# A streaming encoder layer on eight cores: mixer and attention of the next tile list-scheduled beside the FFN of this one

## What is computed

```python
u, v, gb, gc, xin = split(x @ w_in)            # 5 x 512
v    = layernorm(v, per head of 128)
a    = u * (w_s[h] @ v + b_s[h])               # mixing inside a block of 128 frames, masked
conv = causal width-3 convolution of gc * xin
x = layernorm(ALPHA * x + concat(a, gb * conv) @ w_out)
q = x @ w_q                                    # cross-attention into 256 memory tokens
p = softmax(q @ mem_k.T / 16)
x = layernorm(ALPHA * x + (p @ mem_v) @ w_mem_o)
x = layernorm(ALPHA * x + (silu(x @ w_gate) * (x @ w_up)) @ w_down)
```

## Time and profile before

| | |
|---|---|
| median of 3 runs (lowest, highest) | 4941.5 us (4804.48, 5052.2) |
| profiled execution: its own time | 4957.0 us is its span, slowest core (core 1); the fastest core took 4873.2 |
| TensorE matmul busy | 4037.4 us, 81% |
| TensorE weight load busy | 2823.9 us, 57% (beside the matmuls) |
| VectorE, ScalarE, GpSimd busy | 2130.4, 1153.5, 302.3 us |
| mean granted clock, core 1 | 0.842 |
| DMA | 610.47 MB, mean 123 GB/s |

### The profile page before, as it was taken

How to read it: one execution, slowest core, us unless ns; L and a number is a source line. 1 busy time by engine, 2 the same in 40 slices (tenths; PEclk the granted TensorE clock), 3 DMA queues, 4 the chain that set the end, 5 groups by cost and what they waited for, 6 DMA issues and landing times.

```text
span 4957.0 us, 77469 instructions; the slowest of 8 cores (4873.2 to 4957.0 us)
## 1 busy us (share of the span) xinstructions
PE 4037.4 (81%) x27048; PEld 2823.9 (57%) x27048; DVE 2130.4 (43%) x4671; ACT 1153.5 (23%) x2511; POOL 302.3 (6%) x275
## 2 busy tenths in 40 slices
PE   3476888797979788897879798897979989799794
PEld 2254565565657565665657575655657556575563
DVE  0340544435353545445353545445154441544423
ACT  1020231413222231313122221313122031220312
POOL 1210000000000000000000000000000000000000
PEclk8688889898989899898989899897777777777775
DMA  8899333242424243332424243331423314233135
GB/s 172 136 171 161 124 120 141 88 147 74 177 86 158 94 145 107 115 137 77 158 86 169 83 149 111 116 136 73 149 73 130 115 69 147 76 128 115 64 138 212
DMA packets 137192, 610.47 MB, mean 123 GB/s; under 512 B 26877, under 2 KB 50589, under 8 KB 79724
## 3 DMA queue, kind: packets, MB, share of 16 engines
q1 hardware_dynamic: 90716, 564.31, 32.5%
q0 software_dynamic: 46096, 41.21, 6.6%
HBM read 603.51 MB, written 69.09 MB: 136 GB/s over the span
## 4 chain that ended last, share of the span: by engine, by line
PE 63%; DVE 14%; issue 8%; POOL 4%; ACT 4%; another core or an unknown queue 3%; DMA 3%; DVEq 1%; ACTq 0%; POOLq 0%; SPq 0%
PE bank L710 13%; PE bank L680 12%; PE bank L685 12%; PE bank L545 8%; PE bank L458 6%; PE bank L621 5%; POOL rstd L431 3%; PE bank L650 2%; PE bank L409 2%; ACT PT L643 2%; DVE xbuf L462 2%; DVE acc L516 1%; DMA wsc<-w_in 1%; DMA ring<-wsc 1%
## 5 line engine op out<-in xcount | busy, mean ns | idle before, releaser
L685 PE MATMUL bank<-F,ring 128*128 128x256 bf16 (+1 forms) x5808 | 792.3, 283 | 45.0 <-DMA ring<-wsc 39.0
L680 PE MATMUL bank<-F,ring 128*128 128x256 bf16 (+1 forms) x5808 | 798.7, 285 | 24.6 <-ACT sg L691 21.9
L545 PE MATMUL bank<-F,ring 128*128 128x256 bf16 (+1 forms) x4224 | 534.0, 294 | 206.2 <-DVE acc L516 198.7
L693 DVE TENSOR_TENSOR hT<-bank,sg 128x256 bf16<-128x256 f32 (+1 forms) x726 | 302.1, 418 | 907.8 <-PE bank L685 768.8
L710 PE MATMUL bank<-ring,hT 128*128 128x512 bf16 (+1 forms) x2860 | 672.9, 401 | 18.7 <-DMA ring<-wsc 15.8
L685 PEld LDWEIGHTS bank<-F,ring 128*128 128x128 bf16 x5808 | 583.7, 103 | 136.4 <-issue 49.0
L680 PEld LDWEIGHTS bank<-F,ring 128*128 128x128 bf16 x5808 | 587.9, 103 | 119.2 <-issue 28.2
L545 PEld LDWEIGHTS bank<-F,ring 128*128 128x128 bf16 x4224 | 434.3, 106 | 303.4 <-issue 224.1
L412 ACT ACTIVATE F<-bank 128x512 bf16<-128x512 f32 (+1 forms) x390 | 231.0, 594 | 1526.3 <-PE bank L409 1510.9
L710 PEld LDWEIGHTS bank<-ring,hT 128*128 128x128 bf16 (+1 forms) x2860 | 291.4, 102 | 393.5 <-issue 168.9
L409 PE MATMUL bank<-ident,xbuf 128*128 128x128 f32 (+1 forms) x1560 | 269.2, 334 | 291.8 <-DVE xbuf L448 234.8
(11 more groups left out here) (135 smaller groups left out, 3111.4 us busy)
## 6 DMA issues: line engine op xcount, KB each, us to landing
ring<-wsc SPq DMA_DIRECT2D x446, 1024.0 KB, 5.5
xbuf<-x_prompt SPq DMA_DIRECT2D x16, 2048.0 KB, 12.6
y_prompt<-xbuf SPq DMA_DIRECT2D x64, 512.0 KB, 2.9
ring<-wsc SPq DMA_DIRECT2D x51, 512.0 KB, 5.2
wsc<-w_gate POOLq DMA_DIRECT2D x5, 1024.0 KB, 108.3
wsc<-w_up POOLq DMA_DIRECT2D x5, 1024.0 KB, 92.5
wsc<-w_down POOLq DMA_DIRECT2D x5, 1024.0 KB, 127.8
wsc<-w_in POOLq DMA_DIRECT2D x16, 256.0 KB, 5.3
```

The lines of the kernel that those rows point to most:

```text
L545: op("tensor", lambda e, bk=bk, g=g, kc=kc, rg=rg: e.matmul(bk[:, 0:Tn], lhsT=rg[:, kc * 512 + g * 128:kc * 512 + (g + 1) * 128], rhs=F0[: ...
L680: op("tensor", lambda e, bkg=bkg, m=m, kc=kc, rgg=rgg, rl=rl: e.matmul(bkg[:, 0:Tn], lhsT=rgg[:, kc * rl + m * 128:kc * rl + (m + 1) * 128 ...
L685: op("tensor", lambda e, bku=bku, m=m, kc=kc, rgu=rgu, rl=rl: e.matmul(bku[:, 0:Tn], lhsT=rgu[:, kc * rl + m * 128:kc * rl + (m + 1) * 128 ...
L693: op("vector", lambda e, bku=bku, sgs=sgs, f=f: e.tensor_tensor(out=hT[:, f, cs], in0=bku[:, 0:Tn], in1=sgs, op=ALU.mult), reads=[bbu2, bs ...
```

## The change

The kernel is rewritten around the same arithmetic.

- **Order.** Operations are recorded with a duration, a priority and their buffers; `Sched.order()` then plays a list schedule and fixes from it, before the program is built, each engine's order. Part A of a tile (mixer and attention) has priority from t - 0.3 on, part B (the FFN) of tile t from t + 1, so that part A of tile t+1 stands among the matmuls of part B of tile t. Each part has its own weight ring (3 and 4 slots) and its own 4 PSUM banks.
- **Width.** All matmuls on a prompt tile stream 512 columns (the mixing inside blocks: 128).
- **Memory.** Once at the start, `precompute` folds the keys into the query weights and the values into the output weights, per group: the scores are then one projection of x of width 1,024 (`scores`), and after the softmax (`norm_p`) one projection gives the output. `w_q`, `K`, `V` and `w_mem_o` are no longer touched in the tiles.
- **Transposes.** x arrives a second time, already turned, as an input of its own (`x_prompt_t`), loaded by a cast DMA from GpSimd. The other two transposes of a tile are a bf16 copy by ScalarE and four DMA transposes on SyncE (`to_feature`, 128 x 1,024 bf16 each, 256 KB), into F0 (for the scores) and F2 (for the FFN).
- **Weights.** In the first use a piece is cast from the float32 input straight into its ring slot and stored from there to `wsc`; later uses read `wsc`. The input's pieces are laid out so that each partition's 4,096 columns are contiguous.
- **Sample.** The 64 sample frames go through tile 0's stages on the same weight pieces.
- The spatial bias, the layer norm of v and the convolution are rearranged (bias folded into one table, normalisation on ScalarE).

```diff
+    def order(self):
...
+            o = heapq.heappop(ready[e])[2]
...
+            if o.dma:
+                occ = 1.0 if e == "gpsimd" else 0.08
+                start = max(t + occ + 0.6, dma_free)
+                dma_free = start + o.nbytes / 330e3
+                fin = dma_free + 1.8
+            else:
+                occ = o.dur
+                if e == "scalar" and o.table is not None:
+                    if table is not None and o.table != table:
+                        occ += 1.4
+                    table = o.table
+                fin = t + occ
...
+        NRA, NRB = 3, 4
+        ring = {"A": [T("ra%d" % i, [128, 4096], BF16) for i in range(NRA)],
+                "B": [T("rb%d" % i, [128, 4096], BF16) for i in range(NRB)]}
...
+        pool = {"A": [0, 1, 2, 3], "B": [4, 5, 6, 7]}
...
+        def c_mm(n, cols):
+            return n * max(0.056, (cols + 6) / 2400.0)
...
+            if name in sidx and name in stored:
+                src = wsc[sidx[name]]
+                op("sync", lambda e: e.dma_start(out=t[:, 0:nco], in_=src[:, 0:nco]), [buf("wsc_" + name)], [b],
+                   dma="r%s%d" % (r, i), nbytes=256 * nco, dprio=dprio)
+            else:
+                src = wp[widx[name]]
+                op("gpsimd", lambda e: e.dma_start(out=t[:, 0:nco], in_=src[:, 0:nco]), [], [b],
+                   dma="f%s%d" % (r, i), nbytes=512 * nco, dprio=dprio)
+                if name in sidx:
+                    dst = wsc[sidx[name]]
+                    op("sync", lambda e: e.dma_start(out=dst[:, 0:nco], in_=t[:, 0:nco]), [b], [buf("wsc_" + name)],
+                       dma="w%s%d" % (r, i), nbytes=256 * nco, dprio=dprio)
+                    stored.add(name)
+            return t, b
...
+        def load_x(t):
+            i = t % 2
+            op("gpsimd", lambda e: e.dma_start(out=F0[:], in_=xpT[:, t]), [], [buf("F0_%d" % s) for s in range(4)],
+               dma="xt", nbytes=1 << 21, dprio=-0.25)
+            op("sync", lambda e: e.dma_start(out=xbuf[i][:], in_=xp[t * TT:(t + 1) * TT, :].rearrange("(s p) d -> p s d", p=128)),
+               [], [buf("x%d_%d" % (i, s)) for s in range(4)], dma="x%d" % i, nbytes=1 << 21, dprio=-0.1)
...
-        def transposes_to_feat(xb_i, subs, SP, c0, FT, b_FT):
-            for j, s in enumerate(subs):
-                for g in range(2):
-                    bk, bb = next_bank()
-                    for c4 in range(4):
-                        c = g * 4 + c4
-                        op("tensor", lambda e, bk=bk, s=s, c=c, c4=c4: e.transpose(
-                            bk[:, c4 * SP:(c4 + 1) * SP], xbuf[xb_i][0:SP, s, c * 128:(c + 1) * 128], ident[0:SP, 0:SP]),
-                           reads=[b_xb[xb_i][s], buf("ident")], writes=[bb])
-                    op("scalar", lambda e, bk=bk, j=j, g=g: e.activation(
-                        out=FT[:, g * 4:(g + 1) * 4, c0 + j * SP:c0 + (j + 1) * SP],
-                        in_=bk[:, 0:4 * SP].rearrange("p (c t) -> p c t", c=4), func=AF.Copy),
-                       reads=[bb], writes=[b_FT])
...
+        def resid(bk, bb, xv, bx, half, SP, i):
+
+            sl = slice(half * 512, (half + 1) * 512)
+            V(lambda e: e.scalar_tensor_tensor(out=xv[:, sl], in0=xv[:, sl], scalar=ALPHA, in1=bk[0:SP, :],
+                                               op0=ALU.mult, op1=ALU.add), [bb, bx[half]], [bx[half]], 512)
+            V(lambda e: e.bn_stats(out=stat[i][0:SP, half, :], in_=xv[:, sl]), [bx[half]], [buf("stat%d" % i)], 512)
+
+        def ln_apply(xv, bx, SP, li, i):
+            V(lambda e: e.bn_aggr(out=mv[i][0:SP, 0, :], in_=stat[i][0:SP, 0:2, :].rearrange("p a b -> p (a b)")),
+              [buf("stat%d" % i)], [buf("mv%d" % i)], 12)
+            rsqrt_stats(i, SP, 1)
+            V(lambda e: e.scalar_tensor_tensor(out=xv, in0=xv, scalar=mv[i][0:SP, 0, 0:1], in1=lng[li][0:SP, :],
+                                               op0=ALU.subtract, op1=ALU.mult), bx + [buf("mv%d" % i), buf("lng%d" % li)], bx, 1024)
+            V(lambda e: e.scalar_tensor_tensor(out=xv, in0=xv, scalar=rs[i][0:SP, 0:1], in1=lnb[li][0:SP, :],
+                                               op0=ALU.mult, op1=ALU.add), bx + [buf("rs%d" % i), buf("lnb%d" % li)], bx, 1024)
+
+        def to_feature(xv, bx, SP, dst, b_dst):
+
+            j = rot("xb", NXB)
+            A(lambda e: e.activation(out=xb[j][0:SP, :], in_=xv, func=AF.Copy), bx, [buf("xb%d" % j)], 1024)
+            op("sync", lambda e: e.dma_start_transpose(out=dst, in_=xb[j][0:SP, :]), [buf("xb%d" % j)], [b_dst],
+               dma="tr%d" % j, nbytes=1 << 19)
...
+                    MM([(bk[:], rg[:, k * 512 + cc * 128:k * 512 + (cc + 1) * 128], F0[:, k, :], k == 0, k == 7) for k in range(8)],
+                       [buf("F0_%d" % s) for s in range(4)] + [brg], [bb], 512)
+                    A(lambda e, bk=bk, ch=ch: e.activation(out=F1[:, ch, :], in_=bk[:], func=AF.Exp, scale=1.0 / 16.0),
+                      [bb], [buf("F1_%d" % ch)], 512, table="exp")
+                norm_p(F1, "F1_", h, TT)
+        def norm_p(FT, bn, h, n):
+            bk, bb = bank("A")
+            MM([(bk[:, 0:n], ones_bf[:], FT[:, 2 * h + mc, :], mc == 0, mc == 1) for mc in range(2)],
+               [buf("ones"), buf(bn + str(2 * h)), buf(bn + str(2 * h + 1))], [bb], n)
+            A(lambda e: e.activation(out=rden[:, 0:n], in_=bk[:, 0:n], func=AF.Ln), [bb], [buf("rden")], n, table="exp")
+            A(lambda e: e.activation(out=rden[:, 0:n], in_=rden[:, 0:n], func=AF.Exp, scale=-1.0), [buf("rden")], [buf("rden")], n, table="exp")
+            for mc in range(2):
+                V(lambda e, mc=mc: e.tensor_tensor(out=FT[:, 2 * h + mc, :], in0=FT[:, 2 * h + mc, :], in1=rden[:, 0:n], op=ALU.mult),
+                  [buf("rden"), buf(bn + str(2 * h + mc))], [buf(bn + str(2 * h + mc))], n)
...
+                        MM([(bk[:, i * 256:(i + 1) * 256], rg[:, (4 * hp + 2 * i + dc) * 512 + kk * 128:(4 * hp + 2 * i + dc) * 512 + (kk + 1) * 128],
+                             KT[z][:, 4 * hp + 2 * i + dc, :], dc == 0, dc == 1) for i in range(2) for dc in range(2)],
+                           [brg, b_KT[z]], [bb], 256)
...
+        def run_A(tiles, t):
+            def at(f):
+                S.prio = t + f - OFF
+            p_main = tiles[-1]
+            at(0.0)
+            rg, brg = piece("A", "in_v")
+            for c in tiles:
+                in_proj_v(c, rg, brg)
+            for m in range(4):
...
+                at(0.65 + 0.1 * hp)
...
+                at(0.86 + 0.07 * half)
...
+        def run_B(tiles, t):
+            n = NF // 2
+            for j in range(n):
+                S.prio = t + 1.0 + 0.6 * j / n
+                rg, brg = piece("B", "gu%d" % j)
+                for c in tiles:
+                    gate_up(c, j, rg, brg)
...
+                    S.prio = t + 1.6 + 0.2 * half + 0.06 * kp
```

More of the change, by code:

```diff
@@ L1 @@
 import contextlib
+import heapq
 import numpy as np
@@ L40, in __init__, with op @@
         self.sig = 0
-        self.dma = dma
+        self.dma = stream is not None
         self.stream = stream
         self.cnt = 0
+        self.dur = dur
+        self.prio = prio
+        self.nbytes = nbytes
+        self.seq = seq
+        self.left = 0
+        self.est = 0.0
+        self.fin = 0.0
+        self.succ = []
+        self.table = table
 class Sched:
+    LAT = 0.20
+    LAT_TO_PE = 0.45
     def __init__(self, nc):
         self.nc = nc
[L48 to L56, removed]
+        self.ops = []
+        self.prio = 0.0
+    def op(self, eng, fn, reads=(), writes=(), dma=None, dur=0.1, nbytes=0, table=None, dprio=0.0):
+        o = Op(eng, fn, dma, dur, self.prio + dprio, nbytes, len(self.ops), table)
         deps = []
@@ L84, in emit @@
     def emit(self, final_wait_eng="sync"):
         nc = self.nc
+        q = self.order()
+        streams = {}
         for e in QUEUES:
-            for o in self.q[e]:
+            for o in q[e]:
+                if o.dma:
+                    streams.setdefault(o.stream, []).append(o)
+        total = {}
+        for s, os_ in streams.items():
+            os_.sort(key=lambda o: o.seq)
+            for i, o in enumerate(os_):
+                o.cnt = 16 * (i + 1)
+            total[s] = 16 * len(os_)
@@ L88, in emit @@
+        for e in QUEUES:
+            for o in q[e]:
                 best = {}
@@ L103, in emit @@
             c = 0
[L104 to L107, removed]
+            for o in q[e]:
+                if not o.dma and o.signal:
                     c += 1
@@ new lines, in to_feature, with prompt_tile @@
+        def to_feature(xv, bx, SP, dst, b_dst):
[3 more added lines that the diff above has]
+               dma="tr%d" % j, nbytes=1 << 19)
+        class Tile:
+            pass
+        def prompt_tile(t):
+            c = Tile()
+            c.sample = False
+            c.t = t
+            i = t % 2
+            c.x = [xbuf[i][:, s, :] for s in range(4)]
```

(14 more changed lines are left out.)

1243 lines of the change are left out of this document (565 added, 678 removed).

## The result

The changed kernel takes 3,475.49 us in the median; the runs of both that can be compared give a ratio of 0.7231, with 95% between 0.7214 and 0.7247. The forecast was 3,530. (One of the four runs of the changed kernel took 3,862.23 us, with die 1's cores at a mean clock of 0.87, and the median of the kernel before, 4,996.85 beside these runs, holds runs of this kind too; the ratio leaves them out on both sides and is against some 4,805.)

The account below looks back on a forecast made before the run. Bounds differed by stage: TensorE in the FFN, waits in mixer and attention, DMA at the start. Stream 3,093, sample and folding 135, start 130, tile 1 60, steady waits 70 and end 22 led to 3,530; range 3,350 to 3,950.

Parts of the forecast that it names:

- the 20 for the clock: Whole program: 20 us for a lower clock, known only from the reflection; the prediction's text does not list it.
- the steady tiles: 14 tiles with part A among the FFN's matmuls: 5 us of wait each, 70 us in all (0 to 280).
- tile 1: Tile 1's part A, with no earlier tile's FFN beside it: 60 us of waits and half-clock matmuls (30 to 110).
- the end: After the last tile's matmuls: final layer norm and the store, 22 us.
- the start: Until tile 0's FFN is through: casts and plain transfers take 477 us, leaving TensorE 130 us idle.
- the sum of 27: Ahead of a steady tile's scores: layer norm, copy and DMA transpose take 27 us, against 27.7 us of covering matmuls.
- Sample, 167 at the end: The separate sample tile's 167 us at the end go; its matmuls move into tile 0.
- Width and weight loads at nothing: In the tiles, weight loads cost nothing, some 110 of 193 us; 512-column matmuls priced at 0.2167 us each.
- The transposes' rival: Steady tiles: DMA transposes run one after another near 10 us each, 20 us of wait in 14 tiles; 3,850, chance 0.12.
- the formula decided from 22: Slower-than-before rival: two transpose waits of together 8T - 80 us a tile, slower from T = 22 us; chance 0.04.
- The order holds: Opposite of a rival: engine orders fixed from assumed durations fail, part A hides only in part; 4,060, chance 0.06.
- The rival of the clock: Dense stretches: the low clock, 0.81, stays; 3,780 if as long as now, 4,060 if throughout; chance 0.2, half each.

Follow-up runs that it names:

- The longer program: Changed kernel with its tile loop run over twice (32 tiles, the second 16 on the same data): 6,626.62 us profiled, 7,173.86 in a second run.
- the first experiment: Changed kernel with part A of a tile ranked behind part B of the tile before: 4,166.99 us, ratio 0.8663 to the kernel before.

## Why the prediction was right

- **The sum.** TensorE's work was put at 3,228 us and is 3,245.6. The price of a matmul takes off 12. The sample's 608 small matmuls were priced by their own length, 0.072 us, and not by their share of a stream: 32 of them with 64 columns stand from 413.75 to 414.69 us, 0.029 each, and that takes off 26. What comes on top is the lower clock of three of the four stretches: 11% of 329, 9% of 158 and 9% of 58.5 us are about 55. Idle time was put at 282 and is 229.
- **Luck in it.** Work, idle time and the 20 for the clock make up the difference of 55 us, but errors of both signs stand in it: the steady tiles 70 too high, tile 1 18, the clock 20, the end 6; the start 41 too low, the work 18. The 20 rested on cores of a die that start some 3,450 us apart, read from two stretches "of the same length" that are 1,507 and some 1,675 us long. The longer program shows another distance, if it is one; that 1.00 held in the runs compared was not foreseen by a mechanism that any run shows.
- **Start, 130 taken:** 171 idle in the first 500 us, inside its bounds of 50 to 285. It is not transfers alone: DMA's share was to be near 1 and is 0.85, with 0.55 between 300 and 400 us, where TensorE idles too. Some 20 us were a queue that stood behind the guard, and most of the sample's work is on the path.
- **Tile 1's part A, 60 taken:** 42. A like amount, 39, returns in every tile of the first experiment, where nothing covers part A.
- **Steady tiles, 70 taken:** 0. This is the term that was mis-sized most. The mechanism held: the cover of 27.7 us was right (27.6), and the chain under it fits, as the sum of 27 said. The 5 us a tile put on top of that sum did not come, and the chain is 23.6: in the tile shown a transpose lands after 3.3 us, not 5.3 (4.2 in the median of all), and the blocks follow at 3.7, not 4.4. The Trainium skill, "DMA: Bandwidth & Descriptors", section "Latency and other measured facts", gives an effective 261 GB/s, an estimate of 1 us for 256 KB; the 3.0 us of the shortest show that at this size the rate is not the price.
- **Sample, 167 at the end:** gone, as said, but with the sample last instead of merged it is 12 to 21 us only.
- **Width and weight loads at nothing:** 256 columns cost 34 us, 1% of the time; no wait for weights shows in the steady tiles.
- **Rivals.** The transposes' rival had its formula right for the scores and its price wrong; at 19 us each the kernel is slower than before, at 5,044 us, where the formula decided from 22. The order holds in the tiles and failed at one place at the start, behind a late DMA. The rival of the clock is not refuted: 1.00 stands in the profiled run, and what decides between it and 0.81 was not found.

The step that held most was that part A finds its cover: 692 us. That DMA transposes would be cheap was needed for it only in so far as they fit under it.

## What to carry to other kernels

Place a latency-bound stage beside another tile's dense one before taking work out of it: the same DMA transposes gained nothing in the old order and are free in the new one. Then write down, at the tightest place, the chain in VectorE steps and landings against the matmuls between, since what does not fit comes back in every tile. An operation that waits for a late transfer belongs on no queue on which another stage's short operations stand.

## What the runs showed of the hardware

- A DMA transpose of 128 x 1,024 bf16 within SBUF took 3.0 to 8.1 us from issue to landing, 4.2 in the median, over the 112 between 700 and 3,400 us of the changed kernel, beside 186 GB/s of traffic in the mean. Each held SyncE's queue for 1.24 us in the median.
- The granted clock was 1.00 on all eight cores in the stretches read between 420 and 3,400 us of the changed kernel's profiled run where TensorE is dense. The Trainium skill, "TensorE: Matmul & The Clock Gate", Part 1, has a die fall to 13/16 once three of its cores are dense. The traces agree in the level: 0.81 stands in the longer program on cores 0 and 1 early and on 2 and 3 late. They do not show how many cores were dense at once, since no row has the cores' starts against each other; eight cores in one launch were not enough for it. What sets it stays open.
